# Softmax division moved from the probabilities to the attention outputs, in two of three attentions, with one block copy in four on VectorE

## The reference, cut to what matters

```python
s = jnp.einsum('bqkgd,bskd->bkgqs', q_blk, k_blk) * scale + bias      # layer 0: windows of +-128, a sink
p = jax.nn.softmax(jnp.concatenate([s, sink_l], axis=-1), axis=-1)[..., :SPAN]
out = jnp.einsum('bkgqs,bskd->bqkgd', p, v_blk)
...
p = jax.nn.softmax(s.reshape(B, B_HEADS, GRID_W, kr * kc), axis=-1)   # layer 1: a neighbourhood in a grid
out = jnp.einsum('bhwrc,brwchd->bwhd', p, v_nb)
...
p = jax.nn.softmax(s, axis=-1)                                        # both layers: 4 heads over 256 memory slots
return jnp.einsum('bhsm,bmhd->bshd', p, mv)
```

## Time and profile before

| | |
|---|---|
| median of 3 runs | 1915.92 us (1914.45 to 1915.96) |
| profiled execution | 1916.02 us, its span 1914.2 us |
| TensorE busy | 1896.0 us, 99% of the span, 10458 products |
| VectorE busy | 963.2 us, 50% |
| ScalarE busy | 772.5 us, 40% |
| GpSimd busy | 182.6 us, 10% |
| granted TensorE clock | 0.998 of full, in all slices 9 tenths or more |
| chain that ended last | 88% TensorE, 4% ScalarE, 4% VectorE |

### The profile page before, as it was taken

One profiled execution on the slowest core, in us unless ns is written; L12 is line 12 of the kernel. 1 busy time (PEld: TensorE's weight loads), 2 busy tenths in 40 slices (PEclk: granted clock), 3 DMA queues, 4 the chain that ended last, 5 costly groups with the idle time before them and its releaser, 6 DMA issues.

```text
span 1914.2 us, 25105 instructions
## 1 busy us (share of the span) xinstructions
PE 1896.0 (99%) x10458; PEld 1566.7 (82%) x10458; DVE 963.2 (50%) x1497; ACT 772.5 (40%) x1251; POOL 182.6 (10%) x196
## 2 busy tenths in 40 slices
PE   9999999999999999999999999999999999999998
PEld 7878888888888867888888888878887888888887
DVE  5693665553245274566553236443655555325532
ACT  5494433333333285433323324333764443212321
POOL 4112200000005041300000103000000020000000
PEclk9999999999999999999999999999999999999999
DMA  6512233334333311223333332331212333233222
GB/s 191 197 35 77 78 99 99 96 93 143 92 106 117 99 46 56 88 91 97 99 99 91 102 105 99 99 111 57 61 37 86 116 90 97 99 99 97 92 98 88
DMA packets 54136, 182.96 MB, mean 96 GB/s; under 512 B 6604, under 2 KB 10060, under 8 KB 53512
## 3 DMA queue, kind: packets, MB, share of 16 engines
q1 hardware_dynamic: 51528, 172.28, 28.6%
q0 software_dynamic: 2352, 9.02, 1.6%
q10 hardware_dynamic: 144, 0.06, 0.0%
HBM read 176.58 MB, written 4.76 MB: 95 GB/s over the span
## 4 chain that ended last, share of the span: by engine, by line
PE 88%; ACT 4%; DVE 4%; issue 1%; DMA 1%; POOL 1%; SPq 0%; DVEq 0%; ACTq 0%
PE bank L1889 22%; PE bank L1891 22%; PE bank L1890 22%; PE bank L1908 2%; PE bank L1909 2%; PE bank L1910 2%; ACT prob_long L834 1%; PE bank L2139 1%; ACT pt_short L823 1%; PE bank L1669 1%; PE bank L1672 1%; PE bank L1677 1%; PE bank L1968 1%; PE bank L1967 1%; PE bank L1969 1%
## 5 line engine op out<-in xcount | busy, mean ns | idle before, releaser
L1141 DVE TENSOR_TENSOR w_lo<-w_raw,w_hi 128x1024 fp32r<-128x1024 f32 (+3 forms) x319 | 388.2, 1219 | 710.4 <-ACT w_hi L647 710.2
L647 ACT CAST w_hi<-w_raw 128x1024 fp32r<-128x1024 f32 (+3 forms) x319 | 321.9, 1010 | 552.2 <-DMA w_raw<-in_w_down 131.6
L1889 PE MATMUL bank<-h_hi,w_hi 128*128 128x512 f32 x1272 | 496.4, 390 | 0.8 <-DVE w_lo L1141 0.5
L1890 PE MATMUL bank<-h_lo,w_hi 128*128 128x512 f32 x1272 | 495.7, 390 | 0.0
L1891 PE MATMUL bank<-h_hi,w_lo 128*128 128x512 f32 x1272 | 495.7, 390 | 0.0
L1889 PEld LDWEIGHTS bank<-h_hi,w_hi 128*128 128x128 f32 x1272 | 239.2, 188 | 52.9 <-issue 2.2
L1891 PEld LDWEIGHTS bank<-h_hi,w_lo 128*128 128x128 f32 x1272 | 239.2, 188 | 50.2
L1890 PEld LDWEIGHTS bank<-h_lo,w_hi 128*128 128x128 f32 x1272 | 239.1, 188 | 49.3
L1889 PE MATMUL bank<-a_hi,w_hi 128*128 128x512 f32 (+1 forms) x676 | 261.5, 387 | 0.0
L1890 PE MATMUL bank<-a_lo,w_hi 128*128 128x512 f32 (+1 forms) x676 | 261.3, 387 | 0.0
L1891 PE MATMUL bank<-a_hi,w_lo 128*128 128x512 f32 (+1 forms) x676 | 261.3, 386 | 0.0
(11 more groups left out here) (328 smaller groups left out, 2550.5 us busy)
## 6 DMA issues: line engine op xcount, KB each, us to landing
w_raw<-in_w_gu SPq DMA_DIRECT2D x87, 512.0 KB, 3.5
w_raw<-in_w_mlp_in SPq DMA_DIRECT2D x32, 512.0 KB, 3.5
w_raw<-in_w_mlp_out SPq DMA_DIRECT2D x32, 512.0 KB, 3.6
w_raw<-in_w_down SPq DMA_DIRECT2D x32, 448.0 KB, 3.3
w_raw<-in_w_out SPq DMA_DIRECT2D x24, 512.0 KB, 3.5
w_raw<-in_w_down SPq DMA_DIRECT2D x16, 512.0 KB, 3.5
w_raw<-in_w_gates SPq DMA_DIRECT2D x16, 512.0 KB, 3.5
w_raw<-in_w_qk_b SPq DMA_DIRECT2D x14, 512.0 KB, 3.6
```

What stands on the lines that cost most here:

```text
L647: nc.scalar.copy(hi_of(v), raw_of(v)).then_inc(w_hi_done, 1)
L1141: nc.vector.tensor_tensor(lo_of(v), raw_of(v), hi_of(v).bitcast(F32), ALU.subtract).then_inc(w_split, 1)
L1889: mm(acc, w1, hi, start=start, stop=False)
L1890: mm(acc, w1, lo, start=False, stop=False)
```

## The change

In phases 0 and 1 the probabilities are no longer divided by their sums. The exponentials are turned and multiplied with the values as they are, and the output of a pair of heads is multiplied by the reciprocals of the sums. The output is transposed (queries along the columns), while the sums lie along the partitions, so the reciprocals have to be turned as well:

- The sums of a pair's four steps go to one column of `sums` for each of two pairs in turn. After the masking of the next pair's first step, VectorE makes one reciprocal for the pair, from eight sums, each repeated 64 times, into 512 columns of `raw`. It does so at `s - 1` = last step of the pair.
- TensorE turns these 512 columns with eight more transposes, together with the blocks of step 4, 8, ..., 32, three rounds later, into the upper half of banks 4 and 5. There is one more call of `turn`, for `d` = 32, which only turns the last pair's reciprocals.
- ScalarE copies both in one instruction (`turned_blocks` gives the range of blocks: 8 instead of 4 at these steps). `copy_output` is gone in phases 0 and 1.
- VectorE makes the copy for steps 2, 6, 10, ... (`by_vector`), after the masking of round `s = d + 3`.
- For a pair's output VectorE now makes a product (bank times turned reciprocals, into `act_out`), the rounded part from it and the remainder, each waiting for the one before. This stays in round `s` = last step of the pair + 5.
- TensorE's transposes wait for the exponentials (`p_exp`) and no longer for the scaled probabilities (`p_ready`). The bank of an output is free after the product (`o_scaled`).
- The tensor `den` and its code are gone; no step has more than one piece.

```diff
             def copy_turned(phase, d, steps):
+                if by_vector(phase, d, steps):
+                    turned[0] += 1
+                    return
                 if d >= 2:
                     act.wait_ge(pv_done, pv[0] + d - 1)
                 act.wait_ge(t_ready, turned[0] + 1)
-                n = 2 * len(steps[d].blocks)
-                dst = pt_of(phase, d)[:, :P * n].rearrange("p (n r q) -> p r n q", n=n, r=2)
-                src = turn_banks[:, :, :64 * n].rearrange("p r (n q) -> p r n q", n=n)
+                begin, end = turned_blocks(phase, d, steps)
+                dst = pt_of(phase, d)[:, P * begin:P * end].rearrange("p (n r q) -> p r n q", n=end - begin, r=2)
+                src = turn_banks[:, :, 64 * begin:64 * end].rearrange("p r (n q) -> p r n q", n=end - begin)
                 nc.scalar.activation(dst, src, ACT.Copy).then_inc(pt_copied, 1)
...
                     st = steps[d]
                     o_count[0] += 1
+                    acc = bank_in(phase, 6 + st.pair_no % 2)[:, :]
+                    if phase < 2:
+                        dve.wait_ge(pt_copied, turned[0] + d + 2)
+                        dve.wait_ge(pv_done, pv[0] + d + 1)
+                        o = act_out[:, st.pair_no % 2, :]
+                        nc.vector.tensor_tensor(o, acc, pt_of(phase, d + 1)[:, 4 * P:8 * P], ALU.mult).then_inc(o_scaled, 1)
+                        dve.wait_ge(o_scaled, o_count[0])
+                        nc.vector.tensor_copy(o_hi[:, st.pair, :], o).then_inc(o_hi_done, 1)
+                        dve.wait_ge(o_hi_done, o_count[0])
+                        nc.vector.tensor_tensor(o_lo[:, st.pair, :], o, o_hi[:, st.pair, :].bitcast(F32),
+                                                ALU.subtract).then_inc(o_ready, 1)
+                        return
...
+                    d = s - LAG_T[phase]
+                    if 0 <= d < n and by_vector(phase, d, steps):
+                        dve.wait_ge(pv_done, pv[0] + d - 1)
+                        dve.wait_ge(t_ready, turned[0] + d + 1)
+                        m = 2 * len(steps[d].blocks)
+                        dst = pt_of(phase, d)[:, :P * m].rearrange("p (n r q) -> p r n q", n=m, r=2)
+                        src = turn_banks[:, :, :64 * m].rearrange("p r (n q) -> p r n q", n=m)
+                        nc.vector.tensor_copy(dst, src).then_inc(pt_copied, 1)
                     d = s - 1
                     if 0 <= d < n:
...
+                        if phase < 2 and steps[d].last:
+                            dve.wait_ge(p_exp, expd[0])
+                            of = steps[d].pair_no % 2
+                            total = sums[:, :, :, of:of + 1].rearrange("p i h o -> p (i h) o").to_broadcast([P, 8, HD])
+                            nc.vector.reciprocal(raw[:, of, :].rearrange("p (n d) -> p n d", n=8), total).then_inc(rden_done, 1)
+                            rdens[0] += 1
...
-                    pe.wait_ge(p_ready, ready[0])
+                    pe.wait_ge(p_exp if phase < 2 else p_ready, ready[0])
...
+                if phase < 2 and d and d % 4 == 0:
+                    pe.wait_ge(rden_done, heads[0] + d // 4)
+                    for i in range(4):
+                        for part in range(2):
+                            last = nc.tensor.transpose(ps[4 + part][:, 256 + 64 * i:256 + 64 * i + 64],
+                                                       raw[rows(part), (d // 4 - 1) % 2, P * i:P * i + P],
+                                                       ident[rows(part), 64 * part:64 * part + 64])
                 last.then_inc(t_ready, 1)
```

More of the change, by code:

```diff
@@ L833, in exps @@
                         part = prob_of(phase, s, half)[:, p["at"]:p["at"] + p["width"]]
+                        of = st.pair_no % 2 if phase < 2 else k
                         nc.scalar.activation(part, part, ACT.Exp, bias=top, scale=-1.0,
-                                             accum_out=sums[:, s % 4, half, k:k + 1]).then_inc(p_exp, 1)
+                                             accum_out=sums[:, s % 4, half, of:of + 1]).then_inc(p_exp, 1)
                 masked[0] += 2 * m
@@ L841, in copy_output @@
                 act.wait_ge(pv_done, pv[0] + d + 1)
-                dst, src = o_hi[:, steps[d].pair, :], bank_in(phase, 6 + steps[d].pair_no % 2)[:, :]
-                if phase == 2:
-                    dst, src = unclassed(dst, src)
+                dst, src = unclassed(o_hi[:, steps[d].pair, :], bank_in(phase, 6 + steps[d].pair_no % 2)[:, :])
                 nc.scalar.copy(dst, src).then_inc(o_hi_done, 1)
@@ L1318, in softmax @@
[L1318 to L1322, removed]
-                            nc.vector.tensor_scalar(part, part, rden[:, i, half:half + 1], None, ALU.mult).then_inc(p_ready, 1)
+                        expd[0] += 2
+                        if phase < 2 and steps[d].last:
[4 more added lines that the diff above has]
+                            rdens[0] += 1
+                        elif phase == 2:
+                            dve.wait_ge(p_exp, expd[0])
+                            nc.vector.reciprocal(rden[:, d % 4, :], sums[:, d % 4, :, 0]).then_inc(rden_done, 1)
+                            rdens[0] += 1
+                            dve.wait_ge(rden_done, rdens[0])
+                            for half in range(2):
+                                part = prob_of(phase, d, half)[:, :steps[d].width]
+                                nc.vector.tensor_scalar(part, part, rden[:, d % 4, half:half + 1], None, ALU.mult).then_inc(p_ready, 1)
@@ L1335, in softmax @@
                     output_remainder(n - 1)
[L1336 to L1338 removed]
+                turned[0] += n + 1 if phase < 2 else n
+                pv[0] += n
+            masked, expd, rdens, o_count, turned, pv = [0], [0], [0], [0], [0], [0]
             def bias_load(phase, pair, half):
@@ L2047, in turn @@
                     wait_reads((act_read, 0, 0))
-                if not 0 <= d < len(steps):
+                if not (0 <= d < len(steps) or phase < 2 and d == len(steps)):
                     return
-                blocks = steps[d].blocks
                 if turned[0]:
                     pe.wait_ge(pt_copied, turned[0])
-                for half in range(2):
+                for half in range(2 if d < len(steps) else 0):
+                    blocks = steps[d].blocks
                     ready[0] += 1
-                    pe.wait_ge(p_ready, ready[0])
+                    pe.wait_ge(p_exp if phase < 2 else p_ready, ready[0])
                     first_key = steps[d].pieces[0][half]["first_key"]
@@ L2120, in softmax @@
                         pe.wait_ge(pt_copied, copied[0])
-                        banks = 1 if phase == 2 else 2
-                        if st.first and st.pair_no >= banks:
-                            pe.wait_ge(o_ready, heads[0] + st.pair_no - banks + 1)
+                        if st.first and phase < 2 and st.pair_no >= 2:
+                            pe.wait_ge(o_scaled, heads[0] + st.pair_no - 1)
+                        elif st.first and phase == 2 and st.pair_no:
+                            pe.wait_ge(o_ready, heads[0] + st.pair_no)
                         n_v = len(st.vs[0])
```

29 lines of the change are left out of this document (8 added, 21 removed).

## The result

| | before | after |
|---|---|---|
| time, median (range), us | 1915.94 (1914.45 to 1917.19), 4 runs | 2003.41 (2002.67 to 2006.29), 4 runs |
| profiled execution: time, span, us | 1916.0, 1914.2 | 2002.67, 2000.8 |
| TensorE's granted clock, mean | 0.998 | 0.972 |
| TensorE, VectorE, ScalarE busy | 99%, 50%, 40% | 97%, 50%, 38% |

After / before is 1.0461, 95% interval [1.0447, 1.0474]: slower by 87.5 us. The forecast was 1934 with a range of 1919 to 1990. It had the sign and the place, and was wrong in the size by 69 us.

The account below looks back on a forecast made before the run. TensorE, 99% busy, bounds the kernel, with ScalarE holding it back slightly; VectorE's chain to its block copy would stall it. First attention 9.7 plus second 8.2 made 17.9 us on 1916.0: 1934, range 1919 to 1990.

Parts of the forecast that it names:

- I take 0.60: VectorE's wide reciprocal at step 0 of a pair, 512 columns: assumed 0.60 us, the step of an ordinary instruction.
- two fits of the 160 ns: Bounds for VectorE's 512-column reciprocal: fixed part 0.16 gives 0.43 to 0.69 us; fixed part 0.136 gives 6.3 us.
- rival (a): VectorE's wide reciprocal is dear and lengthens the chain: 1972 us at 6 ns a column, 1948 at 3; chance 0.28.
- the two readings that the prediction weighed: Reciprocal's repeat count of 8: eight times 1.04 ns a column, 4.3 us and 1989; or stages passed once, the forecast.
- 31 + 4.6 + 2 = 38: Extra for a 3.2 us reciprocal: 31 for twelve pairs, 4.6 for each attention's second pair, some 2 at the tails.
- The sign that the prediction named for a dear reciprocal: TensorE before the block transposes: if the second pair of an attention stalls too, the reciprocal is dear.
- The chain and its order: VectorE from step 0's scores through output work to step 1's block copy: 5.27 us against TensorE's 3.82, stall 1.45.
- ScalarE's relief: ScalarE loses the output rounding and one block copy in four; costed at nothing, as TensorE waits for VectorE's copy.
- the forecast's own case: First attention with a 0.60 us reciprocal: TensorE stalls 1.45 us, a pair takes 8.67 us; chance 0.43.
- Rival (b): At step 2's transposes VectorE's block copy is not late, only sums count: 1913 us, not slower; chance 0.16.
- GpSimd's share: Second attention, GpSimd mask additions slow VectorE's new rounding and remainder: 0.5 us for each of three pairs, 1.5.

Follow-up runs that it names:

- filled kernels: Unused TensorE multiplications fill each pair's stall: twelve added to the change, 1982.98 us; five added to the kernel with the narrow reciprocal, 1938.4 us.
- narrow reciprocal: Against the changed kernel, the reciprocal is made of the 8 sums only and a copy spreads it over 512 columns: 1941.61 us.

## Why the prediction was wrong

**The step that failed** is a term of the sum, "The reciprocal over 512 columns is shown nowhere; see below, I take 0.60". It measured 3.35 us. Of the two fits of the 160 ns for two columns, the one with a fixed part of 0.136 and several ns a column was right in kind, and its 12 ns (6.3 us) twice too much; now 203 ns for 8 and 3350 for 512 give 6.24 ns a column and 0.15 us fixed. That is rival (a) at its middle price of 6 ns, to which the prediction gave 0.28. The argument for 0.60, that an addition of two columns would take just 160 ns, was weak: two columns hide any price a column up to 12 ns. The Trainium skill, "VectorE: DVE Perf Modes", section "Walkthrough: the 8-slice pipeline in each mode", has a reciprocal as an iterative divide with a repeat count of 8. The measurement stands between the two readings that the prediction weighed: 6.0 times the 1.04 ns a column of an addition, neither 8 nor 1.

**A second part was missing.** No term and no rival had TensorE's clock in it. Rival (a) with the right price came to 1972, 31 us short. The stalls of 4 us were followed by stretches at 1.2 GHz, and this cost 18.5 us.

**The account**, by the differences to the kernel before on the same chip, with the filled kernels, so that the clock stands in one term only: the change with the narrow reciprocal +23.8 (1938.4 - 1914.6); the wide one in its place, 69.0 - 23.8 = +45.2; the clock, 87.5 - 69.0 = +18.5; together 87.5. The medians of the kernel before differ by up to 2 us from chip to chip, so each term is good to some 2 us.

- *The 23.8* were forecast as 17.9. Unfilled, the narrow kernel's first attention was nearly right: the dense product behind it starts 11.3 us later than before the change (170.41 against 159.12), where 9.7 were forecast. The second took 15.6 (771.47 against 744.54, less the 11.3), where 8.2 were forecast. In the profiled execution with the stall filled, the fastest of its four, the two are 11.8 and 10.3 (170.90 and 766.65): in the second attention most of the excess was the clock, and some 2 us are left in each. They were not taken apart further.
- *The 45.2* were given by the rival as 31 + 4.6 + 2 = 38 at 3.2 us, 7 too few; why is not shown. The sign that the prediction named for a dear reciprocal is there: the second pair of an attention stalls too, 2.10 us in the first attention and 2.19 in the second, by the same block copy.
- *The 18.5* were forecast as nothing.

With its own price right, rival (a) was short of the result by these three: 5.9, 7.2 and 18.5 us.

**What was right.** The chain and its order, each price in it but one (within 0.04 us), the place of the stall (transposes of step 2, released by VectorE's block copy), ScalarE's relief worth nothing there, eight more transposes at 0.24 us (in the narrow kernel sixteen take 0.59, 100.97 to 101.56, where eight took 0.34), and the pair of the forecast's own case: 8.67 said, 8.86 measured. Rival (b), that the copy is not late, needed a chain of 3.8 us: with the output's work and the reciprocal out of the way that state was built, and it gave 1921.3 and 1915.0, where (b) said 1913. GpSimd's share, 1.5 us in the sum, can be read in the narrow kernel with the filled stall. In the second attention the remainder takes 0.96 us while GpSimd adds masks and 0.69 otherwise, in three pairs, and one rounding 0.11 longer. That is some 0.9 us, and 0.27 to 0.38 a pair: that the whole excess of 0.8 comes back on the new instructions is not borne out.

```profile
711.98 4.48 POOL L619 TENSOR_TENSOR bias_grid<-bias_grid,grid_masks 128x192 f32<-128x192 f32 x6 [1.76 <-DMA bias_grid<-in_rpb]
712.34 0.96 DVE L1291 TENSOR_TENSOR h_lo<-act_out,h_hi 128x512 fp32r<-128x512 f32 x1
...
728.66 0.69 DVE L1291 TENSOR_TENSOR h_lo<-act_out,h_hi 128x512 fp32r<-128x512 f32 x1
```

## What to carry to other kernels

Where an operation's price is known for a handful of columns only, the fixed part hides the price a column; then take the dear case as the forecast's equal, and compute what is needed on the few distinct values before spreading them by a copy (0.20 + 0.43 us here against 3.35). Work that is equal in sum can still cost 26 us (2 to 3 of them the clock) if it all lies in one step between a masking and a copy that another engine waits for; spread over the steps it cost 6, and nothing with that copy on the other engine. And a stall that comes back every few us is to be costed twice, once as idle time and once as the time in which TensorE may run at its lower clock behind it (18.5 us here on top of 69.0).

## What the hardware showed unexpectedly

- VectorE's reciprocal: 160 ns for 2 columns, 203 for 8, 1752 for 256, 3350 for 512 (fp32). A subtraction of 512 columns took 0.69 us.
- TensorE's clock: in the first attention of the change, with stalls of 3.88 to 4.34 us from the third pair on, it was 0.74 to 0.87 in the windows of 13 us; in the second, where the stalls were 1.38 to 4.22 us, it was 0.50 to 0.81 in windows of 15 us. With the same chain and 2.94 us of the stalls filled by twelve unused multiplications it was 1.00 in most windows (0.87 and 0.89 in the others) and the kernel 18.5 us faster. With the narrow reciprocal and stalls of 1.24 us a pair it stayed at 1.00 in the first attention; in the second, with stalls of 0.45 to 1.77, it fell to 0.77 and 0.89 in windows of 15 us:

```profile
705.00:720.00 15.00, 13.48 (x150) 9.39 (x152) 9.32 (x40) 10.67 (x34) 9.39 (x15) 0.77 0.09 22
720.00:735.00 15.00, 11.78 (x140) 8.27 (x140) 10.22 (x36) 9.34 (x31) 4.20 (x6) 0.89 0.05 16
```
